# Spreading the mLSTM row bounds over the partitions: a round trip through DRAM, or selector products on TensorE

## The reference, in what matters

```
lf = log_sigmoid(f_pre);  bcum = cumsum(lf)
dmat = bcum[q] - bcum[k] + ig[k]          (k <= q)
m_t  = max(a_inter, max_k dmat)
w_intra = exp(dmat - m_t)
hout = num / max(|den|, exp(-m_t))
```

## Time and profile before

| | us |
|---|---|
| median of 3 runs (lowest, highest) | 986.77 (986.6, 987.88) |
| the profiled execution | 986.77 |
| its span, first to last instruction | 984.9 |
| TensorE busy | 905.7 |
| VectorE busy | 479.7 |
| ScalarE busy | 330.1 |
| GpSimd busy | 193.4 |

### The profile page before, as it was taken

How to read it: one execution, slowest core, us unless ns; L and a number is a source line. 1 busy time by engine, 2 the same in 40 slices (tenths; PEclk the granted TensorE clock), 3 DMA queues, 4 the chain that set the end, 5 groups by cost and what they waited for, 6 DMA issues and landing times.

```text
span 984.9 us, 11757 instructions
## 1 busy us (share of the span) xinstructions
PE 905.7 (92%) x4622; PEld 641.9 (65%) x4622; DVE 479.7 (49%) x969; ACT 330.1 (34%) x548; POOL 193.4 (20%) x169
## 2 busy tenths in 40 slices
PE   5999999999999988999999999985999987778496
PEld 4788788778878856888888854553555543334375
DVE  6378678669758969533333312271111111111655
ACT  5544353553435366322222101120212111112564
POOL 0052263344327221000000000002233322221000
PEclk9999999999999999999999999997999999999799
DMA  7430321222120202622222067399999999997801
GB/s 265 171 95 13 128 65 43 107 65 65 47 104 1 81 17 88 276 96 96 96 96 96 1 249 307 107 397 344 409 420 419 420 420 421 420 419 302 318 29 64
DMA packets 29806, 186.61 MB, mean 189 GB/s; under 512 B 5920, under 2 KB 6432, under 8 KB 19256
## 3 DMA queue, kind: packets, MB, share of 16 engines
q1 hardware_dynamic: 24632, 177.45, 45.9%
q0 software_dynamic: 5120, 8.41, 2.3%
HBM read 177.43 MB, written 16.79 MB: 197 GB/s over the span
## 4 chain that ended last, share of the span: by engine, by line
PE 75%; DMA 14%; DVE 6%; ACT 2%; issue 1%; SPq 1%; DVEq 0%; POOLq 0%; ACTq 0%
PE bank L1024 72%; DMA arena<-in_w_expert 8%; DMA yT<-in_w_expert 3%; PE bank L1357 1%; DMA mT<-normed,table 1%; PE bank L1114 1%; PE bank L1282 1%; DMA x_sb<-in_x 1%; DVE x_sb L1941 1%; DVE pg_low L1918 0%; SPq L530 0%; DVE x_sb L1940 0%; DMA arena<-expert_rows 0%; PE bank L1375 0%; DVE yT L1715 0%
## 5 line engine op out<-in xcount | busy, mean ns | idle before, releaser
L1024 PE MATMUL bank<-mT_parts,low_parts 128*128 128x512 f32 (+1 forms) x456 | 179.2, 395 | 0.0
L1024 PE MATMUL bank<-arena,cst 128*64 128x256 f32 (+2 forms) x936 | 137.7, 434 | 20.1 <-DMA arena<-in_w_expert 12.3
L1024 PE MATMUL bank<-arena 128*128 128x64 f32 (+8 forms) x528 | 135.8, 396 | 4.6 <-ACT arena L729 1.8
L1024 PE MATMUL bank<-mT_parts,x_parts 128*128 128x512 f32 (+1 forms) x328 | 132.9, 405 | 0.0
L1024 PE MATMUL bank<-hT_parts,x_parts 128*128 128x512 f32 (+1 forms) x328 | 129.6, 395 | 0.0
L1895 DVE TENSOR_TENSOR cst<-bank,chn 128x512 f32<-128x512 f32 x32 | 22.1, 691 | 196.2 <-PE bank L1357 196.2
L1024 PEld LDWEIGHTS bank<-arena,cst 128*64 128x64 f32 (+1 forms) x936 | 65.7, 141 | 78.4 <-issue 29.7
L1024 PEld LDWEIGHTS bank<-arena 128*128 128x128 f32 (+1 forms) x528 | 80.4, 189 | 55.0 <-issue 45.7
L1518 DVE TENSOR_TENSOR low_parts<-arena,x_parts 128x1024 fp32r<-128x1024 f32 (+1 forms) x44 | 62.7, 1426 | 96.9 <-ACT x_parts L664 96.6
L1024 PEld LDWEIGHTS bank<-mT_parts,low_parts 128*128 128x128 f32 (+1 forms) x456 | 85.3, 187 | 21.3
L1570 DVE SCALAR_TENSOR_TENSOR arena<-arena,chn 128x512 f32<-128x512 f32 x116 | 99.1, 911 | 0.0
(11 more groups left out here) (269 smaller groups left out, 1431.4 us busy)
## 6 DMA issues: line engine op xcount, KB each, us to landing
arena<-in_w_expert SPq DMA_DIRECT2D x24, 2048.0 KB
arena<-in_w_expert SPq DMA_DIRECT2D x20, 1024.0 KB
arena<-in_w_cm SPq DMA_DIRECT2D x32, 512.0 KB, 3.6
arena<-in_w_gate SPq DMA_DIRECT2D x8, 1536.0 KB, 6.6
x_sb<-in_w_expert SPq DMA_DIRECT2D x8, 1024.0 KB
yT<-in_w_expert SPq DMA_DIRECT2D x4, 2048.0 KB
hT<-in_w_expert SPq DMA_DIRECT2D x4, 2048.0 KB
arena<-in_w_tm SPq DMA_DIRECT2D x4, 1536.0 KB, 7.3
```

The costliest lines, as they stand in the source:

```text
L1024: return pe.matmul(out, lhsT, rhs, start=start, stop=stop)
```

## The change

The DRAM tensor and both transfers go, and with them SyncE's waits on `prefix_ready` and `bound_moved`; its weight loads stand in one plain loop in the same order. In their place TensorE multiplies the four rows with a selector (the constant `sel`: for head h a 4 x 128 matrix whose row h is ones and whose other rows are zero), which puts row h into all 128 partitions of a bank: four plain float32 products of 128 x 512, one for each head, into S_1, S_4, S_16 and OUT, between tiles 2 and 3. VectorE copies the four banks to `mb` behind the low part of tile 3 and ahead of that of tile 4. `mb_ready` counts the four copies and the copy of `ecol`; GpSimd's start and TensorE's units of round 0 wait for all five. The first two steps of the gate arithmetic count on `if_ready` now, so that `prefix_ready` has other values with the same meaning.

```diff
-            column_weights(0, 4)
-            token_weights(0)
-            column_weights(0, 5)
-            sp.wait_ge(prefix_ready, 6)
-            sp.dma_start(bound_rows.rearrange("(h s) -> h s", h=4), rows[0:4, 2, :]).then_inc(bound_moved, 16)
-            column_weights(0, 6)
-            sp.wait_ge(bound_moved, 16)
-            sp.dma_start(mb.rearrange("p h s -> p (h s)"), bound_rows.partition_broadcast(P)).then_inc(bound_moved, 16)
-            column_weights(0, 7)
...
+            for r in range(ROUNDS):
+                for n in range(0 if r else 4, CM_ORDER):
                     column_weights(r, n)
                     if n == 4:
-                        token_weights(r)
+                        sp.wait_ge(if_projected, 1)
+                        sp.dma_start(wtm, w_tm[r, :, :, :]).then_inc(tm_loaded, 16)
...
-                act.wait_ge(prefix_ready, 7)
+                act.wait_ge(prefix_ready, 5)
...
+            def spread_gates():
+
+                pe.wait_ge(consts_loaded, 16)
+                pe.wait_ge(prefix_ready, 4)
+                for h in range(4):
+                    last = mm((S_1, S_4, S_16, OUT)[h][:, :], const("sel", 4)[:, h * P:(h + 1) * P], rows[0:4, 2, :])
+                last.then_inc(gates_step, 1)
...
-                    pe.wait_ge(columns_read, 1)
+                    pe.wait_ge(mb_ready, 5)
...
             column_tile(0, 2)
+            spread_gates()
             column_tile(0, 3)
...
             cm_tile(0, 3)
+            dve.wait_ge(gates_step, 1)
+            for h in range(4):
+                dve.tensor_copy(mb[:, h, :], (S_1, S_4, S_16, OUT)[h][:, :]).then_inc(mb_ready, 1)
             cm_tile(0, 4)
-            dve.wait_ge(gates_step, 1)
+            dve.wait_ge(gates_step, 2)
...
-            pool.wait_ge(columns_read, 1)
-            pool.wait_ge(bound_moved, 32)
+            pool.wait_ge(mb_ready, 5)
```

More of the change, by code:

```diff
@@ L127, in build @@
     x2_rows = nc.dram_tensor("x2_rows", [SEQ, D], F32, kind="Internal").ap()
-    bound_rows = nc.dram_tensor("bound_rows", [4 * SEQ], F32, kind="Internal").ap()
     pple_rows = nc.dram_tensor("pple_rows", [SEQ, D], F32, kind="Internal").ap()
@@ L340, in build @@
         if_projected = sem("if_projected")
+        if_ready = sem("if_ready")
         gates_step = sem("gates_step")
@@ L347, in build @@
         prefix_ready = sem("prefix_ready")
-        columns_read = sem("columns_read")
-        bound_moved = sem("bound_moved")
+        mb_ready = sem("mb_ready")
         cm_loaded = [sem(f"cm_loaded{s}") for s in range(4)]
@@ L491, in _ @@
                 sp.dma_start(dst, src).then_inc(params_loaded, 16)
-            def token_weights(r):
-                sp.wait_ge(if_projected, 1)
-                sp.dma_start(wtm, w_tm[r, :, :, :]).then_inc(tm_loaded, 16)
-            column_weights(0, 4)
-            token_weights(0)
-            column_weights(0, 5)
-            sp.wait_ge(prefix_ready, 6)
-            sp.dma_start(bound_rows.rearrange("(h s) -> h s", h=4), rows[0:4, 2, :]).then_inc(bound_moved, 16)
-            column_weights(0, 6)
-            sp.wait_ge(bound_moved, 16)
-            sp.dma_start(mb.rearrange("p h s -> p (h s)"), bound_rows.partition_broadcast(P)).then_inc(bound_moved, 16)
-            column_weights(0, 7)
-            for r in range(1, ROUNDS):
-                for n in range(CM_ORDER):
+            for r in range(ROUNDS):
+                for n in range(0 if r else 4, CM_ORDER):
                     column_weights(r, n)
                     if n == 4:
-                        token_weights(r)
+                        sp.wait_ge(if_projected, 1)
+                        sp.dma_start(wtm, w_tm[r, :, :, :]).then_inc(tm_loaded, 16)
             def gate_weights(slot, dt):
@@ L1540, in _ @@
             dve.wait_ge(if_projected, 1)
-            dve.tensor_scalar(if_sum[0:4, :], MM[0:4, :], chn[0:4, IF_BIAS:IF_BIAS + 1], None, ALU.add).then_inc(prefix_ready, 1)
+            dve.tensor_scalar(if_sum[0:4, :], MM[0:4, :], chn[0:4, IF_BIAS:IF_BIAS + 1], None, ALU.add).then_inc(if_ready, 1)
             dve.wait_ge(act_step, 4)
             dve.scalar_tensor_tensor(rows[0:4, 2, :], forget[0:4, :], 0.0, forget_log[0:4, :], ALU.min, ALU.subtract)\
-               .then_inc(prefix_ready, 1)
+               .then_inc(if_ready, 1)
+            dve.wait_ge(if_ready, 2)
+            dve.tensor_tensor_scan(rows[0:4, 3, :], rows[0:4, 0, :], rows[0:4, 2, :], 0.0, ALU.mult, ALU.add).then_inc(prefix_ready, 1)
+            dve.wait_ge(prefix_ready, 1)
+            dve.tensor_tensor(rows[0:4, 1, :], if_sum[0:4, :], rows[0:4, 3, :], ALU.subtract).then_inc(prefix_ready, 1)
             dve.wait_ge(prefix_ready, 2)
-            dve.tensor_tensor_scan(rows[0:4, 3, :], rows[0:4, 0, :], rows[0:4, 2, :], 0.0, ALU.mult, ALU.add).then_inc(prefix_ready, 1)
-            dve.wait_ge(prefix_ready, 3)
-            dve.tensor_tensor(rows[0:4, 1, :], if_sum[0:4, :], rows[0:4, 3, :], ALU.subtract).then_inc(prefix_ready, 1)
+            dve.tensor_tensor_scan(rows[0:4, 2, :], rows[0:4, 1, :], rows[0:4, 1, :], 0.0, ALU.max, ALU.max).then_inc(prefix_ready, 2)
             dve.wait_ge(prefix_ready, 4)
-            dve.tensor_tensor_scan(rows[0:4, 2, :], rows[0:4, 1, :], rows[0:4, 1, :], 0.0, ALU.max, ALU.max).then_inc(prefix_ready, 2)
-            dve.wait_ge(prefix_ready, 6)
             dve.tensor_tensor(rows[0:4, 3, :], rows[0:4, 3, :], rows[0:4, 2, :], ALU.add).then_inc(prefix_ready, 1)
             cm_tile(0, 3)
+            dve.wait_ge(gates_step, 1)
+            for h in range(4):
+                dve.tensor_copy(mb[:, h, :], (S_1, S_4, S_16, OUT)[h][:, :]).then_inc(mb_ready, 1)
             cm_tile(0, 4)
-            dve.wait_ge(gates_step, 1)
+            dve.wait_ge(gates_step, 2)
             dve.tensor_copy(ucol[:, :, :], TR[:, 0:16].rearrange("p (t h) -> p t h", t=T))
-            dve.tensor_copy(ecol[:, :, :], TR[:, 16:32].rearrange("p (t h) -> p t h", t=T)).then_inc(columns_read, 1)
+            dve.tensor_copy(ecol[:, :, :], TR[:, 16:32].rearrange("p (t h) -> p t h", t=T)).then_inc(mb_ready, 1)
             def conv_steps(r, first, end):
```

## The result

The changed kernel took 992.91 us (median of 6 runs, 990.77 to 993.56), the kernel before 986.71 us (6 runs, 985.74 to 987.88): a ratio of 1.0053, 95% interval 1.0034 to 1.0073. (The medians alone give 1.0063; the record lists 14 executions of the changed kernel, 988.46 to 995.78 us with a median of 992.07, and the ratio fits these.) Measured again beside the variants, it took 991.21 us (5 runs) against 987.32 (22 runs), a ratio of 1.0037 (1.0023 to 1.0051). Forecast were 990.2 us and a range up to 991.6. The sign was right; the first measurement lies above the range, the second inside it. The profiled execution took 992.15 us, with a span of 990.0.

A forecast was written before the change was run, and what follows sets the result against it. TensorE was taken as the bound where the change sits. Eight records of 3.51 us from 42.83 move tile 3 from 42.93 to 46.34, a shift of 3.41, everything else nothing: 986.77 + 3.41 = 990.2 us, range 988.7 to 991.6.

The forecast's parts named there:

- TensorE bounds the place, and what is laid into its queue is paid in full: At 40 to 60 us TensorE is busy 19.98 of 20.00; work added there moves everything behind it.
- the end: End of the kernel: every later stage follows TensorE, so the whole 3.41 us shift arrives there.
- The transfers' removal and the waits on SyncE are worth nothing: Around 43 us, round 0: TensorE doesn't wait for the broadcast; at most 0.1 us comes back.
- Eight records at 0.43 us, a shift of 3.41: Between tiles 2 and 3: four products take 3.51 us, moving tile 3 from 42.93 to 46.34 us.
- the entry: TensorE going from rounded to plain products before tile 3: a step of 0.32 us, first pass at 42.83.
- the stall of tile 3: TensorE's start of tile 3, late for VectorE's low part: a wait of about 0.2 us that goes away.
- Weight loads beside the passes: In the added products: loads overlap the passes as in `conv_mean`; otherwise the shift would be some 4.5 us.
- VectorE's copies hidden, margin over 2 us: VectorE between the low parts of tiles 3 and 4: four copies, 2.7 us, cost nothing.
- The step that failed: Added products and tile 3: TensorE's granted clock assumed to stay at 1.00.
- the rivals gave its fall 4%: Added products and some of tile 3: clock drops to 0.50, 3.4 us more, 993.6 or above; chance 4%.
- The spread of the times: Whole-kernel time: three runs before lie within 1.3 us; 0.5 us allowed for the spread of runs.
- The range of 2.9 us: Whole-kernel time from 988.7 to 991.6 us, leaving out absorption, cheap passes and a dropped clock, 13%.

The follow-up runs named there:

- the variants: The changed kernel with its four products removed, or given other row counts, type, row groups or places; ratios to the kernel before from 0.9997 to 1.0049.
- two stretches: Changed kernel with two four-row products before tile 3 and two behind it; median 990.86 against 986.84 us for the kernel before, ratio 1.0041.

## Why the prediction was wrong
1. *TensorE bounds the place, and what is laid into its queue is paid in full.* Right: without the products the shift is 0.01 us, and tile 4's delay of 6.07 us is still 6.09 at the merge. That "the end" is later by the same held only roughly: 5.1 us there, by later stages that differ between executions.
2. *The transfers' removal and the waits on SyncE are worth nothing.* Right, by the same run.
3. *Eight records at 0.43 us, a shift of 3.41.* Right to 0.12: 3.53 measured at full clock. The records keep their step with four rows, 0.43 us. The nearness is in part luck. I took the entry from a change that was one of rows, 0.32 us in place of an ordinary step of 0.23, which gives the crossing 0.09, and gave nothing to the way out; both together cost 0.4. And I put the stall of tile 3 that goes away at 0.2; its first two steps before, 42.51 to 43.27, take 0.76 in place of 0.46, so 0.3. Eight records of 0.43, and 0.39 less 0.30, are the 3.53; my errors partly cancel. With 128 rows, where there is no such change, the shift is 3.14.
4. *Weight loads beside the passes.* Right: the shift leaves no room for eight loads, and in the changed kernel's second profile they last 0.18 us each and start every 0.43 us, the step of the records:

```profile
43.38 0.18 PEld L1010 LDWEIGHTS bank<-arena,cst 4*128 4x128 f32 x1 [0.24 <-issue]
```

   The Trainium skill ("TensorE: Matmul & The Clock Gate", "The mechanism" of Part 3) has the sentence by which loads on the same row group don't overlap a running matmul; this kernel doesn't bear it out. The same section also lets a load into a background weight buffer go ahead; no run here shows whether these do. The table "Why this matters for your kernels" of the same page of the Trainium skill says that a single matmul over 32 rows takes as long as one over 128, and that matmuls in distinct row groups run concurrently. The trace agrees, with four rows: 0.43 us a record as over 128, and 3.70 us for eight records on the same four rows, 1.14 in four groups.
5. *VectorE's copies hidden, margin over 2 us.* Right: the copies take 2.48 us, and tile 4's low part is done 4.8 us ahead, 2.45 where the clock holds.
6. **The step that failed** is one that the sum took for granted, TensorE's clock at 1.00 through the products and tile 3; the rivals gave its fall 4%: "If four busy rows of 128 count as little work, the passes run at 0.86". They do count as little. The clock fell in three of three profiles, for 3.4 us to 7 us, and took 1.6 to 3.2 us more than the 3.5. My evidence against it was that 64-row products and transposes run at 1.00 in the rounds, a row that ends at 80 us and so holds the 64-row products only from 76 us on. The runs show why it didn't carry over: 64 rows do hold the clock for the whole stretch, four don't, and in the rounds the narrow work stands singly among full-width work, where four-row products too leave it at 1.00. No row of before showed an unbroken stretch of wide four-row work; that should have been a bound with real weight, not a reason to leave it out. The price set for it (6.9 us and above) was an upper one: the fall comes late in the products or behind them.
7. *The spread of the times.* The range of 2.9 us was too narrow. Beside the variants the kernel before itself ran from 984.4 to 989.7 us (25 runs). The profiles show one source of scatter that the sum left out: in 7 of the 20, all of variants, another fall of the clock begins between 346 and 353 us, behind more than 1 us of TensorE's idle time; in the others it doesn't. The profiles give 5.1 to 6.7 us for the change. The measured differences between medians are 6.2 and 3.9 us; the first fits, the second is under it, and its interval (2.3 to 5.0 us) only just misses 5.1. Scatter before tile 1 accounts for some of it: in that profile tile 1 starts 1.3 us earlier than before. A time alone tells the variants with and without the fall poorly apart (1.0041 with 64 rows, 1.0037 for the changed kernel); the granted clock in the profile does.

The Trainium skill's account of the clock ("TensorE: Matmul & The Clock Gate", "What's actually happening" in Part 1) is that a monitor sets it by how busy TensorE has been lately. Here TensorE was busy without a gap by the profile's measure and fell nonetheless; as "busy", a four-row record doesn't count as a 128-row one does, though both last equally long.

Open stays why the fall begins in different places, whether it is in every execution of the changed kernel (it was in three of three) or how often in the one with two stretches (one of two), and from how few rows on it sets in.

## What to carry to other kernels
A product over four rows cost TensorE as much time as one over all 128 here, and a stretch of them halved the clock of what followed; a column of "busy" doesn't warn of it, the granted clock does. Where a few rows have to be spread over the partitions by TensorE, there are three cheaper forms, each of which kept the clock at 1.00 in every profile taken. Padding with zeros to full width costs 3.1 us here in place of 5 to 7, the rounded type of the neighbouring products 1.0 (0.6 with the padding), and side by side in row groups 1.3. With one to three profiles for each, a rarer fall isn't ruled out. And where a transfer does the work beside a saturated TensorE with time to spare, as here, leave it there.

## What was not expected of the hardware
- Zeros hold the clock as well as data does: 124 of 128 rows were zero, and it stayed at 1.00.
- Going over to another number of rows and back costs TensorE 0.4 us for the pair (1.26 against 0.87 us a product); going over between plain and rounded float32 at the same number of rows costs nothing that shows.
- One profile doesn't prove that a clock holds: the kernel with two stretches held it in one profile and lost it in the next.
